# Alternating the candidate search, norms in pieces, and modulation steps moved to the chunk stage, in a two-layer hybrid trunk on one core

## The reference

```python
h = rmsnorm(x, norm1_w) * (1 + sc1) + sh1
u = h @ w_in                       # 2584 columns: SSD, gated DeltaNet, FNet, attention
y = concat(ssd(u), gdn(u), fnet(u), attention(u)) @ w_out
x = x + g1 * y
h2 = rmsnorm(x, norm2_w) * (1 + sc2) + sh2
q = (h2 @ w_q).reshape(t, 8, 2, 128)
s = einsum('thpc,hpkc->thpk', q, sub_keys)            # 16 lists of 128 scores
s_top, i_top = top_k(s, 16)                           # best 16 of each list
cand = s_top[:, :, 0, :, None] + s_top[:, :, 1, None, :]
best, pos = top_k(cand, 16)                           # best 16 pairs of each head
idx = i1[pos] * 128 + i2[pos];  gate = softmax(best)  # 128 experts per token
x = x + g2 * sum_e gate_e * gelu(U[idx_e] . h2) * V[idx_e]
```

## Time and profile before

| | |
|---|---|
| time, median of 3 runs | 2620.67 us (2619.61 to 2624.93) |
| the profiled execution | 2637.35 us, span 2635.6 us |
| busy: TensorE, VectorE, GpSimd, ScalarE | 1741.6, 1563.3, 1452.5, 372.9 us |
| indirect DMAs | 1536 of 512 KB, 805.40 MB of 959.35 MB |
| traffic | 363 GB/s over the span; 420 GB/s in the fullest slices |
| mean granted TensorE clock | 0.831 of full speed |

### The profile page before, as it was taken

How to read it: one execution, slowest core, us unless ns; L and a number is a source line. 1 busy time by engine, 2 the same in 40 slices (tenths; PEclk the granted TensorE clock), 3 DMA queues, 4 the chain that set the end, 5 groups by cost and what they waited for, 6 DMA issues and landing times.

```text
span 2635.6 us, 27950 instructions
## 1 busy us (share of the span) xinstructions
PE 1741.6 (66%) x10250; PEld 1070.4 (41%) x10250; DVE 1563.3 (59%) x4010; ACT 372.9 (14%) x917; POOL 1452.5 (55%) x1540
## 2 busy tenths in 40 slices
PE   6979598778984011079888699868991000088888
PEld 5858477746634011044244188746641000011111
DVE  2314899851689999931108279981499999900000
ACT  3322132121111000010111132211110000000000
POOL 0000455443566676757765645443567777777775
PEclk8989799878996555589999999978995555599999
DMA  9488599766999999999999989866999999999999
GB/s 395 160 326 319 219 421 345 259 227 235 405 410 420 420 420 420 420 361 412 403 415 420 388 330 375 286 226 231 376 411 381 420 420 420 420 420 419 412 420 371
DMA packets 249495, 959.35 MB, mean 364 GB/s; under 512 B 32400, under 2 KB 33680, under 8 KB 231568
## 3 DMA queue, kind: packets, MB, share of 16 engines
q0 software_dynamic: 221184, 805.40, 77.1%
q1 hardware_dynamic: 19584, 142.62, 13.6%
q10 hardware_dynamic: 8592, 9.56, 1.0%
HBM read 955.11 MB, written 2.36 MB: 363 GB/s over the span
## 4 chain that ended last, share of the span: by engine, by line
POOL 26%; PE 24%; DVE 23%; DMA 13%; issue 10%; ACT 2%; ACTq 0%; SPq 0%; POOLq 0%; DVEq 0%
POOL sb_ring L561 26%; PE pb L584 18%; DVE sb_ring L2001 10%; DMA sb_ring<-in_peer_v,sb_idxT 6%; DMA sb_ring<-in_peer_u,sb_idxu 5%; PE pv L584 5%; DMA sb_wring<-in_w_in_blocks 1%; PE pb L587 1%; DVE sb_i16u L1881 1%; DVE sb_big L1572 1%; ACT sb_big L1127 1%; DMA sb_ring<-in_w_mod_blocks 1%; DVE sb_xe L1877 1%; ACT sb_hT L1127 1%; DVE sb_big L1694 1%
## 5 line engine op out<-in xcount | busy, mean ns | idle before, releaser
L561 POOL DMA_INDIRECT sb_ring<-in_peer_u,sb_idxu x768 | 724.7, 944 | 698.7 <-DVE sb_idxT L1969 293.7
L561 POOL DMA_INDIRECT sb_ring<-in_peer_v,sb_idxT x768 | 727.6, 947 | 469.8 <-issue 210.2
L2001 DVE CUSTOM_DVE_ANT_0 sb_ring<-sb_ring,pv 128x1024 f32<-128x1024 f32 x768 | 907.7, 1218 | 29.9 <-DMA sb_ring<-in_peer_u,sb_idxu 22.9
L584 PE MATMUL pv<-sb_ring,sb_wcol 128*32 128x512 f32 x3072 | 645.7, 616 | 75.5 <-DMA sb_ring<-in_peer_v,sb_idxT 67.3
L584 PE MATMUL pb<-sb_hT,sb_wring 128*128 128x256 f32 (+1 forms) x1920 | 372.3, 354 | 49.8 <-ACT sb_big L1127 26.4
L584 PEld LDWEIGHTS pb<-sb_hT,sb_wring 128*128 128x128 f32 x1920 | 319.5, 201 | 122.8 <-issue 73.5
L584 PEld LDWEIGHTS pv<-sb_ring,sb_wcol 128*32 128x32 f32 x3072 | 125.1, 110 | 542.4 <-DMA sb_ring<-in_peer_v,sb_idxT 367.5
L587 PE MATMUL pb<-sb_cst,sb_dots 128*128 128x128 f32 x6 | 2.4, 402 | 409.6 <-DVE sb_dots L2007 409.6
L584 PE MATMUL pb<-sb_big 128*128 128x128 f32 (+1 forms) x1696 | 202.7, 281 | 17.7 <-DVE sb_big L1690 14.2
L584 PEld LDWEIGHTS pb<-sb_big 128*128 128x128 f32 (+1 forms) x1696 | 192.4, 192 | 32.5 <-DVE sb_big L1690 18.0
L2038 DVE TENSOR_TENSOR sb_big<-pv,sb_big 128x512 f32<-128x512 f32 x4 | 2.7, 687 | 318.0 <-PE pv L584 318.0
(11 more groups left out here) (240 smaller groups left out, 1690.0 us busy)
## 6 DMA issues: line engine op xcount, KB each, us to landing
sb_ring<-in_w_mod_blocks SPq DMA_DIRECT2D x38, 1024.0 KB, 7.0
sb_wring<-in_w_in_blocks SPq DMA_DIRECT2D x34, 1024.0 KB, 7.8
sb_wring<-in_w_q_blocks SPq DMA_DIRECT2D x26, 1024.0 KB, 8.0
sb_wring<-in_w_out_blocks SPq DMA_DIRECT2D x14, 1024.0 KB, 7.7
sb_ring<-in_peer_u,sb_idxu POOLq DMA_INDIRECT x768, 10.2
sb_ring<-in_peer_v,sb_idxT POOLq DMA_INDIRECT x768, 8.1
sb_wring<-in_w_mod_blocks SPq DMA_DIRECT2D x10, 1024.0 KB, 7.2
sb_ring<-in_w_in_blocks SPq DMA_DIRECT2D x6, 1024.0 KB, 14.3
```

What stands on the lines that cost most here:

```text
L561: pool.indirect_dma_start(ring[:, j, :], None, a["tab_" + kind][l_of(q)], bass.IndirectOffsetOnAxis(ap=of, axis=0)).then_inc(rows_in[j], 16)
L584: return nc.tensor.matmul(out, lhsT, rhs, start=start, stop=stop)
L2001: dve.tensor_tensor_reduce(out=row, in0=row, in1=pv[:, :, :].rearrange("p a b -> p (a b)"), scale=1.0, scalar=0.0, op0=ALU.mult, op1=ALU.a ...
```

## The change

- `top16`, the search of the lists (`lists`) and `quarter` become generators that pause after each instruction. `st_query` on VectorE runs the lists of set 0 alone; then, for k = 0 to 3, one instruction of `quarter(k)` and one of `lists(k + 1)` in turn. A wait stands ahead of the instruction that needs it and names its own predecessor. The halves z of the last steps of `quarter` get separate waits.
- The scores of set 0 are made before query piece 4, not after it.
- The second norm is in pieces: ScalarE squares each 128-row piece in stage out as soon as it is added, TensorE sums pieces 0 to 5 in out and the last two at the start of query. The first norm is squared in two halves. The product on VectorE is cut into four pairs of pieces, and each pair has its own waits up to TensorE's first matmuls.
- `FIRST_WEAVE`: the steps at gaps of the chunk stage go from 10 to 16 and at its end from 1 to 4; scan has 6 for 5; the end of att0 has 3 for 1; query has none (before: 4 at its first gap and 8 at its end).
- `SAMPLE_WEAVE`: three V steps go from `topk0` (5 to 2) to out (2 to 5).

```diff
-    "scan": ([1, 0, 0, 1, 0, 0, 1, 0], 0), "fnet": ([], 1), "attp": ([1, 1], 0), "att0": ([0, 2, 0], 0), "att1": ([0, 2, 0], 0), "out": ([0, 0, 0, 1, 0, 0, 1], 0),
-    "query": ([3] + [0, 1, 1, 1] * 2 + [1, 1, 1, 1] * 2, 1), "topk0": ([5], 0), "topk1": ([1], 0)}
+    "scan": ([1, 0, 0, 1, 0, 0, 1, 0], 0), "fnet": ([], 1), "attp": ([1, 1], 0), "att0": ([0, 2, 0], 0), "att1": ([0, 2, 0], 0), "out": ([0, 1, 0, 1, 1, 1, 1], 0),
+    "query": ([3] + [0, 1, 1, 1] * 2 + [1, 1, 1, 1] * 2, 1), "topk0": ([2], 0), "topk1": ([1], 0)}
 FIRST_WEAVE = {
-    "intra0": ({k: 1 for k in range(10)}, 1), "scan": ({6: 1, 7: 2}, 2), "fnet": ({}, 1), "attp": ({0: 2}, 1),
-    "att0": ({0: 1, 1: 1, 2: 1}, 1), "out": ({3: 4}, 0), "query": ({0: 4}, 8), "topk0": ({}, 0)}
+    "intra0": ({k: 2 if k < 6 else 1 for k in range(10)}, 4), "scan": ({6: 2, 7: 2}, 2), "fnet": ({}, 1), "attp": ({0: 2}, 1),
+    "att0": ({0: 1, 1: 1, 2: 1}, 3), "out": ({3: 4}, 0), "query": ({}, 0), "topk0": ({}, 0)}
...
+            def sum_square(u, which, c):
+                NC = dims(u)[3]
+                if which:
+                    pe.wait_ge(*done("squares", (u, which, c)))
+                elif c % 4 == 0:
+                    pe.wait_ge(*done("squares", (u, which, c // 4)))
+                if c == 0:
+                    take([0], ("rms_read", (u, which)))
+                last = mm(pb[:, 0, 0:NC], ones, big_at(0, DC, NC)[:, c, :], start=c == 0, stop=c == DC - 1)
...
+                        if j > 1:
+                            sum_square(u, 1, j - 2)
...
+                        if j == 4:
+                            scores(u, 0)
...
+                for pair in range(4):
+                    act.wait_ge(*done("h_normed", (u, which, pair)))
+                    for c in (2 * pair, 2 * pair + 1):
+                        last = fn(hT[:, c, 0:NC], hT[:, c, 0:NC], ACT.Identity, scale=modA[:, l, which, c, g:g + 1],
+                                  bias=modT[:, l, sh + c, g:g + 1])
+                    last.then_inc(*tick("h_ready", (u, which, pair)))
...
+                for _ in lists(u, 0):
+                    pass
+                for k in range(4):
+                    ahead = lists(u, k + 1) if k < 3 else iter(())
+                    for _ in quarter(u, k):
+                        next(ahead, None)
+                    for _ in ahead:
+                        pass
+            def lists(u, k):
...
+                gap(u, "query", 4 * k + 4)
+                for i in range(nt):
+                    dve.wait_ge(*done("s_copied", (u, i, k)))
+                yield from top16(lambda r: scr[r // 4][:, 4 * k + r % 4, :], 4 * nt, lambda r: v16[:, k, r, :], lambda r: i16u[:, r, :])
```

More of the change, by code:

```diff
@@ L647, in sum_squares, with rows_ready @@
                 g, l, nt, NC, c0 = dims(u)
-                pe.wait_ge(*done("squares", (u, which)))
-                take([0], ("rms_read", (u, which)))
                 for c in range(DC):
-                    last = mm(pb[:, 0, 0:NC], ones, big_at(0, DC, NC)[:, c, :], start=c == 0, stop=c == DC - 1)
-                last.then_inc(*tick("rms_full", (u, which)))
+                    sum_square(u, which, c)
+            def sum_square(u, which, c):
[7 more added lines that the diff above has]
+                last = mm(pb[:, 0, 0:NC], ones, big_at(0, DC, NC)[:, c, :], start=c == 0, stop=c == DC - 1)
+                if c == DC - 1:
+                    last.then_inc(*tick("rms_full", (u, which)))
+            def rows_ready(u, which, c):
+                if c % 2 == 0:
+                    pe.wait_ge(*done("h_ready", (u, which, c // 2)))
             def st_load(u):
@@ L699, in st_proj @@
                 g, l, nt, NC, c0 = dims(u)
-                pe.wait_ge(*done("h_ready", (u, 0)))
                 raw_columns(u)
@@ L1419, in st_out @@
                             .then_inc(*tick("yT_copied", ((u, i), k)))
+                if g == 0:
+                    for name in ("out_k", "out_v", "out_ssd", "out_gdn"):
+                        act.wait_ge(sem(name), counts[name])
+                for j in range(8):
+                    square_of(u, j)
+                    gap(u, "out", j)
             def st_query(u):
                 g, l, nt, NC, c0 = dims(u)
-                squares(u, 1)
+                root(u, 1)
                 norm(u, 1)
@@ L1503, in item_final @@
                     act.wait_ge(sem(name), counts[name])
-            stages = {"load": st_load, "norm0": lambda u: squares(u, 0), "norm1": lambda u: norm(u, 0), "proj": st_proj,
+            stages = {"load": st_load, "norm0": squares, "norm1": lambda u: norm(u, 0), "proj": st_proj,
                       "intra0": lambda u: st_intra(u, 0), "intra1": lambda u: st_intra(u, 1), "scan": st_scan,
@@ L1551, in norm @@
                 dve.wait_ge(*stepped())
-                tt(hT[:, :, 0:NC], xT[:, :, c0:c0 + NC], bc1(r, DC), ALU.mult).then_inc(*tick("h_normed", (u, which)))
+                for pair in range(4):
+                    c = slice(2 * pair, 2 * pair + 2)
+                    tt(hT[:, c, 0:NC], xT[:, c, c0:c0 + NC], bc1(r, 2), ALU.mult).then_inc(*tick("h_normed", (u, which, pair)))
                 if not which and u < 2:
@@ L1915, in quarter @@
                 dve.tensor_copy(rise[:, 0:nh, 0:1], num[:, :, 0, 0:1])
[L1916 to L1919, removed]
+                tt(rise[:, 0:nh, 1:16], num[:, :, 0, 1:16], num[:, :, 0, 0:15], ALU.subtract).then_inc(*step())
+                made = stepped()
@@ L1939, in quarter @@
                     halves = ((slice(0, 8), 8), (slice(8, 16), 16))
+                    marked = []
                     for z, m in halves:
[L1941 to L1951, removed]
+                        tt(eq[:, :, z, 0:m], bc2(at[:, :, z], m), bc1(bc1(mark[:, 0:m], 8), nh), pick).then_inc(*step())
+                        marked.append(stepped())
+                        yield
+                    times = []
+                    for (z, m), made in zip(halves, marked):
+                        dve.wait_ge(*made)
+                        tt(eq[:, :, z, 0:m], eq[:, :, z, 0:m], of[:, :, 0:m].unsqueeze(2).to_broadcast((P, nh, 8, m)), ALU.mult) \
+                            .then_inc(*step())
+                        times.append(stepped())
+                        yield
+                    for (z, m), made in zip(halves, times):
+                        dve.wait_ge(*made)
+                        dve.tensor_reduce(out[:, :, z], eq[:, :, z, 0:m], AX_X, ALU.add).then_inc(*step())
+                        made = stepped()
+                        yield
+                    dve.wait_ge(*made)
                 two = hexp[:, :, 0:n].rearrange("p s (i h) -> p s i h", i=nt)
```

114 lines of the change are left out of this document (66 added, 48 removed).

## The result

The change made the kernel slower. Its median is 2635.34 us (2630.79 to 2644.02) against 2621.68 (2614.87 to 2625.33): ratio 1.0056, interval 1.0038 to 1.0075. A second series gave 2638.01 against 2619.63, ratio 1.0076, 1.0060 to 1.0093. So it costs 14 to 18 us by the medians and 15 to 20 by the ratios; the forecast was 2 gained, and 2635 lies 3 above the end of the range.

A forecast was written before the change was run, and what follows sets the result against it. No single engine bounds it; the ends of the searches in u0, u1 and u3 move the time one for one. Changes of 0, -1 and -1 us total -2, from 2620.67 to 2618.5 us; range 2605 to 2632.

The forecast's parts named there:

- Query's start: unchanged.: Samples' query stage: V steps and sums lengthen out, but the norm chain ahead of query shrinks by about as much.
- the V steps' 5.6 and the sums' 2.3: Samples' stage out: three added V steps cost TensorE 5.6 us, and the sums of squares 2.3 us.
- in place of 0.3: All of u0: later modulation steps and out, less savings in query, search and layer 1's sums, end 0.3 us later.
- the credits of 2.0 (a shorter norm chain in u1): In u1, ahead of query: 2.0 us taken off the search's 4.5 us delay for the shorter norm chain.
- 2.4 (backlog): POOL at 772, in u1: earlier V rows remove a backlog of some 2.4 us, counted as a gain.
- Alternation: VectorE's search: 2.7 us saved per set; u0's search 3.8 earlier, samples' 6 later from query's start, 4.5 with clock credit.
- The credit of 1.5 for query's first pieces: Samples' query: first two pieces ran at half clock; keeping TensorE busy before them gains 1.5 us.
- Norms in pieces: Query of u0: first lists 15 us after x, 9.6 earlier; first norm of u3 6 earlier, of u1 1 earlier.
- Modulation steps: In u0: twelve steps leave query and reappear where TensorE sets the pace; out starts 11.7 us later, then adds 2.9.
- the 7.68 for ScalarE's copy: Fold at 158.15 in u0, waiting 7.68 us; ScalarE's DMA issues, and the fold with them, were to shift with the copies.
- late supply: Freed weight blocks or added V steps' rows come late, 3 us each at three or four places: +11, 2630, chance 0.14.
- the prediction's own signs of being wrong: A set below 19 or still 23 us, chunk stage growing much less than 10, or new w_mod or w_out block waits.

The follow-up runs named there:

- the base: Changed kernel with V steps, modulation steps and the samples' search as before; norms in pieces and prompts' alternated search kept: 2591.24 us, 0.9901 of the kernel before.

## Why the prediction was wrong

The step that failed is "Query's start: unchanged." It was 5.0 later in u3. In u1 the first pair of profiles gives 6.3 (595.12 to 649.81 against 600.38 to 648.75), but both hold stretches at the lower clock; the second execution of the changed kernel against the kernel with alternation alone gives 5.4 (52.32 against 46.95). The prediction had the V steps' 5.6 and the sums' 2.3 in out about right (8.3 together), and expected what lies behind out to shrink by as much; it shrank by 3.3. The norm itself did shrink: with one V step ahead of query it takes 5.6 from the start of the last sum, and query's start is unchanged, as forecast (46.9 against 47.0). But the three V steps that had filled the norm's wait at no cost before need 10 there, third step's rows included, and became what query waits for. The wait was taken away and its filling was left in. This much is shown, by the two experiments that take V steps out of TensorE's path. In `topk0` the three steps that were moved cost nothing that shows: with them back there, POOL still idled 8.3 and 9.9 ahead of the next U rows.

Put right by this alone, u1 and u3 come out some 10 later and the forecast at 2629, still inside the range. The rest is an estimate from the stages: u0 came out some 4 later in place of 0.3, the credits of 2.0 (a shorter norm chain in u1) and 2.4 (backlog) were not found, and the samples' searches, from query's start, came out 2.7 longer (u3) in place of 4.5. With these the forecast is about 2633.

Point by point:

- **Alternation.** Right in mechanism and in size: a sample's set was forecast at 20.8 and took 20.6, so 2.8 were saved for 2.7, 0.12 for each wait in place of 0.11. The wait of 15 for the scores of set 1 was 14.05. The sample's search was forecast at 126.5 from query's start and took 124.7, the prompt's at 52.7 and took 51.7. The credit of 1.5 for query's first pieces came out at 1.7 (8.86 to 7.17): before, the granted clock was 0.54 in their first 3.5 us, after an idle time of 3.46, and 0.98 in the rest, so they did not run at half clock throughout; afterwards it was 1.00. For the samples alternation is a loss all the same (5 to 7 each), since a shorter set behind a wait ends later than a longer one that starts at once. "VectorE: DVE Perf Modes", section "The DRAIN you can't avoid", of the Trainium skill says that an operation does not start until the pipe is empty, by which nothing would have been saved; the same section adds that a next operation that is not held starts earlier, which the prediction left out. The trace has a saving, 20.6 against 23.46; no run here shows which instructions were held.
- **Norms in pieces.** Mechanism right, size short: lists 15.6 after x in u0 (15 forecast), softplus 5.2 earlier in u3 (6). What was hardly counted is the second norm of the samples, 7.4 each with the V steps where they were (63.7 in u3 from out's first x to the lists in the base, 71.1 before, as the lines below show; the scores of set 0, made one piece earlier, are part of it). The pieces alone were measured at 22 (18 to 27), from which the 19 of the terms cannot be told apart, though they are made up differently.

```profile
1812.80 0.48 DVE L1870 SCALAR_TENSOR_TENSOR sb_xT<-pb,sb_modT,sb_xT 128x256 f32<-128x256 f32 x1 [8.26 <-PE pb L584]
...
1883.92 0.88 DVE L1877 MAX8 sb_xe<-sb_dec 128x8 f32<-128x128 f32 x4 [32.02 <-ACT sb_cv L1127]
```

- **Modulation steps.** x of u0 14.6 later was forecast, 12.6 was read in the pair of profiles. That the two lie close is luck: before had x at 211.2 in its one profile; with alternation alone, the same instructions up to there, it came at 205.4, in the six others with the old steps at 203 to 208, and in the six with the moved steps at 222 to 226. So x came some 18 later, 17.1 between the base and the base with the steps moved. There the block waits were put at about -2 and were +6.2, while the 7.68 for ScalarE's copy, taken to move along, went; the rest of the difference is open. Taking the four steps out of query gave 1.4. With 18 more here, the lists about 9 earlier after x and the search 4.8 shorter, u0 ends some 4 later.
- **Backlog at 772.** POOL idled 4.80 there, and the V rows left over held up nothing that showed in the time; the 2.4 credited to u1 was not found.
- **The rivals.** Slower had 0.22, most of it for late supply. Late blocks did come, 6 us of them, and the third V step waited 1.77 for its rows; most of the rest came from cover that was gone, which no rival named. TensorE's new waits for w_mod blocks were one of the prediction's own signs of being wrong.

## What to carry to other kernels

When a wait is shortened, look next at the work that was put there to fill it: it is now on the path, and it has to move to where the engine still waits, up to the point where its transfers end last (two more steps moved there cost the base 11 us in the profile). Alternating two dependent chains pays only if the second chain's data are there when the first one is ready to run; else the first is held back by the second's wait. A change of several parts is worth taking apart: here one of them was worth 22 us, and the others gave it all back and more.

## What the runs showed of the hardware

The same instructions ran in u1 at different granted clocks in two executions of the changed kernel. The first, attention's first product and out's first x, and a view of the stretch between (busy us of each engine, then granted clock, DMA share and GB/s):

```profile
555.55 2.85 PE L584 MATMUL pb<-sb_solW 64*128 64x384 f32 x8 [0.84 <-ACT sb_solW L1148]
...
601.28 0.48 DVE L1908 SCALAR_TENSOR_TENSOR sb_xT<-pb,sb_modT,sb_xT 128x256 f32<-128x256 f32 x1 [10.70 <-PE pb L584]
...
555.00:595.00 40.00, 32.24 (x168) 21.43 (x168) 9.72 (x18) 12.99 (x36) 18.19 (x20) 0.68 0.79 286
```

and the second:

```profile
553.74 1.57 PE L584 MATMUL pb<-sb_solW 64*128 64x384 f32 x8 [0.84 <-ACT sb_solW L1148]
...
591.17 0.48 DVE L1908 SCALAR_TENSOR_TENSOR sb_xT<-pb,sb_modT,sb_xT 128x256 f32<-128x256 f32 x1 [6.71 <-PE pb L584]
...
553.00:588.00 35.00, 28.02 (x171) 17.55 (x172) 9.67 (x18) 12.77 (x36) 18.31 (x20) 0.80 0.82 303
```

The granted clock was 0.52 over the 2.85 us of the first product in the first execution, about the lower of the two levels (1.2 GHz), and 1.00 over the 1.57 us in the second, the upper (2.4 GHz). Over the 40 and 35 us viewed it was 0.68 and 0.80, and up to out's first x the executions took 45.7 and 37.4 us; 7.2 of these 8.3 are in TensorE's busy time (38.4 and 31.2). Both executions had come to it through the same instructions, with the same 0.84 us of idle time ahead; what set the level is not shown. So one execution of this kernel differs from the next by 8 us in one stage alone, as much as some of the parts studied here, and a pair of profiles can agree with a sum by chance.
